# Normalised probabilities, transposed attention outputs, and high/low value products over pairs of query tiles

## The chip, the cores and the metric

One core of one Trainium2 chip runs the whole program. The metric is the device time of one execution in microseconds (us). A measurement of this kernel can tell a difference of about 0.2% from none.

## What is computed

Two blocks of two layers each work on 512 tokens with 2048 features, all in float32. The change touches the first block alone, of which each layer is (cut to what matters):

```python
def _layer(x, ...):
    h = _rms_norm(x, g_pre)
    proj = h @ w_in                      # 512 x 2048 by 2048 x 5952
    # a: 8 query heads, 2 key/value heads of 128, normed and rotated (the grouped attention)
    # b: 4 heads, keys and values from a latent of 256
    # c: 4 heads, each query sees 8 x 16 neighbours, with a bias table
    s = q @ k.T * scale
    p = softmax(s)
    o = p @ v
    o_a, o_b, o_c = (o * silu(gate) for each of the three)
    y = concat([o_a, o_b, o_c]) @ w_out  # 512 x 2048 by 2048 x 2048
    return x + _rms_norm(y, g_post)
```

The second block has another mixture (a sliding window, a spatial gate, a gated linear attention) and a modulation vector, `silu(c) @ w_mod`, which GpSimd computes while the first block runs.

## The kernel before

**The dense products.** The weights stream from HBM in panels 512 columns wide (`PW`), each as 8 pieces of two 128-row tiles (`ND`, `KC` = 16 row tiles). ScalarE rounds a piece to fp32r (`split_hi`, L1330), VectorE takes the rest (`split_lo`, L1815), and TensorE makes three matmuls per row tile and 128-token tile: high by low, high by high, low by high (`weights`, L830 to L832; L825 to L827 in the form `turned`, where the weights are the stationary side and the result comes out with features on the partitions). So a step, one row tile of a panel, is 12 matmuls of 512 columns. Panels 0 to 11 of a layer (`NIN` = 12) are `w_in`; panels 12 and on are `w_out`. Panel 2 and 3 are turned; 8 to 11 are the gates.

**The order of the work.** Each engine has its own program, written out by hand, in the same steps. `side1(l, s)` on TensorE, ScalarE and VectorE holds what is done beside the dense product at step s = 16 * panel + row tile. Tables of numbers set the steps: `UNIT_AT` (the attention units), `JOB_AT` (transposes and small products on the way to them), `SUM_AT` (sums of the modulation), `QROPE_A_AT`, `ARSQ_AT`, `ASUM_AT` (query rotation, reciprocal root and sums on VectorE). VectorE and ScalarE run the splits and the side work in one in-order stream: a piece's split, then the sides of two steps (`run`). At a gate panel's end comes `take_gate`: tanh on ScalarE, four multiplications from the banks on VectorE (`gate`, L1919), after which TensorE may use the banks again, and four of `Y` by the gate (`apply`, L1925).

**An attention unit** is one head and one tile of 128 queries; there are 64 in a layer: 16 of b, 16 of c, 32 of a. With s its step in `UNIT_AT`:

- step s: TensorE makes the scores, 128x512 (`score`, L973: three fp32r matmuls in a and c, five in b); VectorE the row maximum (`row_max`, L2109, and in a L2111); ScalarE the exponential into `probs`, with its sum in `sm` (`exp`, L1546).
- step s+2 (`UNIT_TURN`): TensorE transposes `probs` in four pieces into bank 6 (`turn`, L982), ScalarE copies it to `probsT` (`take_turn`, L1554).
- step s+4 (`UNIT_PV`): TensorE multiplies by the values into bank 7, four float32 matmuls of 128 columns with `probsT` as the stationary side (`pv`, L993), which the trace records as eight, two passes each; VectorE takes the reciprocal of the sum and multiplies 128 columns of bank 7 by it into `Y` (`finish`, L2119, L2122).

The units of a stand at steps 125 to 183, in panels 7 to 11, between the two halves' preparation: query rotation (`query_rope`, L2146 to L2152, four at steps 113 to 121, four at 133 to 146), the reciprocal root at steps 124 and 145 (`rsqrt`, L1937 to L1949, and L2264), and one transposing job per head (`job`, L953; `take_job`, L2089 and L2091).

**The output projection.** `Y` has tokens on its partitions. TensorE transposes it, 16 chunks of four 128x128 pieces (`turns_y`, L863): four chunks at step 12 of panel 11, then one in each of the first 12 steps of panel 12. ScalarE and VectorE make `act_hi` and `act_lo` of each chunk from the bank (L1493, L1978).

**GpSimd** runs the modulation (`mod_panel`: L2793 and L2800 on tiles of 512, weights by its own DMA queue) in both layers of the first block. Before panel 6 of it, it waits until the first half of the query rotation is done.

## Time and profile before

| | |
|---|---|
| median of 3 runs | 3445.77 us (3444.96 to 3445.84) |
| the profiled execution's own time | 3441.93 us |
| its span, first to last instruction | 3440.1 us |
| mean granted clock of TensorE | 0.997 of full speed |
| busy: PE, DVE, ACT, POOL | 3393.8, 1883.4, 1296.1, 1161.1 us |

PE is TensorE, DVE is VectorE, ACT is ScalarE, POOL is GpSimd. A matmul's listed length is its latency; what one costs is the distance from its start to the next one's start. In the first layer (by the starts of the first matmuls) panel 7 runs from 442.0 to 494.3 us, panel 8 to 559.7, panel 9 to 627.0, panel 10 to 688.7, panel 11 to 746.9, panel 12 to 796.0.

### The profile page before, as it was taken

How to read it: one execution, taken by the hardware profiler on the slowest of the kernel's cores; microseconds unless marked ns; L12 is line 12 of the kernel's file. 1: busy time of each engine (PE TensorE's matmuls, PEld its weight loads, DVE VectorE, ACT ScalarE, POOL GpSimd, SP SyncE). 2: the span in 40 equal slices, each digit the busy share in tenths (PEclk: the TensorE clock that was granted, in tenths of full speed). 3: DMA queues.
4: the chain of work that ended last, by engine and by line, in shares of the span. 5: the costliest groups of instructions: out<-in, count | busy, mean ns of one | idle time of the engine just before them, and what ended most of it. 6: DMA issues, size and time to landing. Idle time of an engine off the chain costs nothing.

```text
span 3440.1 us, 47703 instructions
## 1 busy us (share of the span) xinstructions
PE 3393.8 (99%) x17660; PEld 2783.0 (81%) x17660; DVE 1883.4 (55%) x3202; ACT 1296.1 (38%) x2125; POOL 1161.1 (34%) x1310
## 2 busy tenths in 40 slices
PE   8999999999999999999999999999999999999998
PEld 7778878888886788888888878877888878887887
DVE  5544577554765347665457445544547535645545
ACT  6133333333641333333347345322236435432233
POOL 0477878754007778786341000001000000001000
PEclk9999999999999999999999999999999999999999
DMA  6455544445664455444557532322446622322345
GB/s 213 147 150 163 149 150 141 145 156 187 201 217 129 141 169 158 145 146 147 167 191 221 159 62 62 101 74 74 147 155 212 186 74 62 95 68 81 123 152 185
DMA packets 225295, 490.53 MB, mean 143 GB/s; under 512 B 24254, under 2 KB 33337, under 8 KB 221224
## 3 DMA queue, kind: packets, MB, share of 16 engines
q1 hardware_dynamic: 188264, 369.13, 34.7%
q0 software_dynamic: 33632, 109.11, 10.7%
q10 hardware_dynamic: 3168, 9.24, 0.8%
q8 instruction: 141, 2.31, 0.3%
q14 instruction: 90, 0.74, 0.1%
HBM read 470.54 MB, written 20.52 MB: 143 GB/s over the span
## 4 chain that ended last, share of the span: by engine, by line
PE 94%; DVE 4%; issue 1%; ACT 1%; DMA 0%; POOL 0%; DVEq 0%; SPq 0%; ACTq 0%
PE bank L830 24%; PE bank L832 23%; PE bank L831 23%; PE bank L993 3%; PE bank L973 3%; PE bank L956 2%; PE bank L825 2%; PE bank L827 2%; PE bank L826 2%; PE bank L982 2%; PE bank L1096 1%; PE bank L1075 1%; PE bank L853 1%; PE bank L863 1%; DVE wlo L1815 1%
## 5 line engine op out<-in xcount | busy, mean ns | idle before, releaser
L830 PE MATMUL bank<-wlo,act_hi 128*128 128x512 f32 (+1 forms) x3712 | 1481.0, 399 | 7.2 <-ACT Y L1409 5.3
L832 PE MATMUL bank<-whi,act_lo 128*128 128x512 f32 (+1 forms) x3712 | 1440.1, 388 | 0.0
L831 PE MATMUL bank<-whi,act_hi 128*128 128x512 f32 (+1 forms) x3712 | 1439.0, 388 | 0.0
L1815 DVE TENSOR_TENSOR wlo<-stage,whi 128x1024 fp32r<-128x1024 f32 (+1 forms) x624 | 814.6, 1308 | 770.0 <-ACT whi L1330 757.0
L1330 ACT ACTIVATE whi<-stage 128x1024 fp32r<-128x1024 f32 (+1 forms) x624 | 649.3, 1041 | 1048.5 <-PE bank L832 899.5
L830 PEld LDWEIGHTS bank<-wlo,act_hi 128*128 128x128 f32 x3712 | 698.4, 188 | 163.6 <-issue 23.7
L832 PEld LDWEIGHTS bank<-whi,act_lo 128*128 128x128 f32 x3712 | 697.9, 188 | 148.0
L831 PEld LDWEIGHTS bank<-whi,act_hi 128*128 128x128 f32 x3712 | 699.3, 188 | 130.3
L2800 POOL TENSOR_TENSOR macc<-macc,mprod 128x512 f32<-128x512 f32 x360 | 508.8, 1413 | 68.2 <-POOL mprod L2793 68.2
L2793 POOL TENSOR_SCALAR mprod<-wmod,csil 128x512 f32<-128x512 f32 x384 | 314.6, 819 | 197.6 <-issue 77.3
L2779 POOL DMA_DIRECT2D wmod<-in_w_mod x384 | 223.2, 581 | 418.9 <-DVE zone L2152 292.3
L2875 POOL TENSOR_TENSOR zone<-zone 128x256 f32<-128x256 f32 x48 | 39.1, 815 | 376.7 <-DVE zone L2602 376.7
L2832 POOL CAST act_hi<-zone 128x256 fp32r<-128x256 f32 x64 | 32.0, 516 | 380.9 <-ACT zone L1485 380.0
L1554 ACT ACTIVATE zone<-bank 128x512 f32<-128x512 f32 x128 | 76.7, 599 | 219.2 <-PE bank L982 218.9
L2857 POOL DMA_DIRECT2D macc<-in_gla_w_gate_up x4 | 2.1, 524 | 431.3 <-DVE Y L2435 431.3
L1546 ACT ACTIVATE zone<-bank,nmx,rsq 128x512 f32<-128x512 f32 x64 | 50.0, 781 | 170.0 <-DVE nmx L2111 170.0
L825 PE MATMUL bank<-act_hi,wlo 128*128 128x512 f32 x256 | 110.0, 430 | 0.0
L2119 DVE RECIPROCAL ri<-sm 128x1 f32<-128x1 f32 x128 | 20.4, 159 | 160.2 <-PE bank L993 159.6
L993 PEld LDWEIGHTS bank<-zone 128*128 128x128 f32 x768 | 100.4, 191 | 7.5
L993 PE MATMUL bank<-zone 128*128 128x128 f32 x768 | 101.0, 274 | 0.0
L827 PE MATMUL bank<-act_lo,whi 128*128 128x512 f32 x256 | 100.1, 391 | 0.0
L826 PE MATMUL bank<-act_hi,whi 128*128 128x512 f32 x256 | 99.8, 390 | 0.0
(282 smaller groups left out, 3177.5 us busy)
## 6 DMA issues: line engine op xcount, KB each, us to landing
stage<-in_w_in SPq DMA_DIRECT2D x400, 512.0 KB, 3.7
wmod<-in_w_mod POOLq DMA_DIRECT2D x384, 256.0 KB, 3.0
stage<-in_w_out SPq DMA_DIRECT2D x192, 512.0 KB, 4.0
out<-Y SPq DMA_DIRECT2D x48, 256.0 KB, 4.7
zone<-out SPq DMA_DIRECT2D x12, 1024.0 KB, 6.6
stage<-in_w_in SPq DMA_DIRECT2D x32, 320.0 KB, 3.2
Y<-in_x SPq DMA_DIRECT2D x4, 1024.0 KB, 9.1
zone<-in_x SPq DMA_DIRECT2D x4, 1024.0 KB, 6.6
```

Of the source, the lines that this page charges most:

```text
L825: pe.matmul(out, lo_w[:, tok(t)], hi_x, start=(k == 0), stop=False)
L826: pe.matmul(out, hi_w[:, tok(t)], hi_x, start=False, stop=False)
L827: mm = pe.matmul(out, hi_w[:, tok(t)], lo_x, start=False, stop=(k == KC - 1))
L830: pe.matmul(out, hi_x, lo_w, start=(k == 0), stop=False)
L831: pe.matmul(out, hi_x, hi_w, start=False, stop=False)
L832: mm = pe.matmul(out, lo_x, hi_w, start=False, stop=(k == KC - 1))
L993: mm = pe.matmul(bank[7][:, 0:HD], probsT[:, u % 2, tok(kt)], values(br, h, kt), start=(kt == 0), stop=(kt == TT - 1))
L1330: act.activation(whi[:, c % RH, :, 0:width], stage[:, c % RS, :, 0:width], ACT.Copy)\
L1815: dve.tensor_tensor(wlo[:, c % RH, :, 0:width], stage[:, c % RS, :, 0:width], whi[:, c % RH, :, 0:width].bitcast(F32), ALU.subtract).then_ ...
L2779: pool.dma_start(wmod[:, k % 2, :], src.rearrange("o p n -> (o p) n")).then_inc(mod_landed[k % 2].sem, 16)
L2793: pool.tensor_scalar(mprod[:, :], wmod[:, k % 2, :], csil[:, k:k + 1], 0.0, ALU.mult, ALU.add)\
L2800: pool.tensor_tensor(macc[:, ring, :], macc[:, ring, :], mprod[:, :], ALU.add).then_inc(mod_added.sem, 1)
```

## The change

In the first block's two layers:

- The probabilities are divided by their sum before they are transposed: `even`, at step s+1 on VectorE, does the reciprocal and one multiplication of `probs`, 128x512, in SBUF. `turn` waits for it. `finish` is a plain copy.
- The value product is made the other way round, values stationary and `probsT` moving, so that bank 7 and then `Y` hold features on the partitions, for all three attentions.
- In a, two units (two query tiles of a head) share one product: the transposed probabilities and the values are each split in a high and a low fp32r part (`turned_low` on VectorE for each unit; `values_high`, `values_low` once in a layer), and 12 fp32r matmuls of 256 columns replace 2 times 4 in float32 (`pv_pair`). It stands one step earlier than the second unit's product did. One copy, `finish_pair`, takes both.
- The gate panels 8 to 11 run `turned`, `apply` walks `Y` in feature tiles, and `turns_y` is gone from the first block: `act_hi` and `act_lo` are made from `Y` in SBUF.
- The second reciprocal root moves from step 145 to 144, the first from 124 to 122; the last query rotation from 146 to 141; GpSimd waits before its panel 6 for the row maximum of a's first unit instead of the query rotation; the post-norm gains are loaded after piece 3 of panel 12 and after the last unit.

```diff
-AQ_AT, ASUM_AT, ARSQ_AT = (113, 131), (116, 132), (124, 145)
-QROPE_A_AT = {113: (0, 0), 115: (0, 1), 119: (0, 2), 121: (0, 3), 133: (1, 0), 136: (1, 1), 139: (1, 2), 146: (1, 3)}
+AQ_AT, ASUM_AT, ARSQ_AT = (113, 131), (116, 132), (122, 144)
+QROPE_A_AT = {113: (0, 0), 115: (0, 1), 119: (0, 2), 121: (0, 3), 133: (1, 0), 136: (1, 1), 139: (1, 2), 141: (1, 3)}
+VALUES_AT = 120, 123
+PV_AT = {}
+for s, u in UNIT_AT.items():
+    if u < U_A:
+        PV_AT[s + UNIT_PV] = (u,)
+    elif u % 2:
+        PV_AT[s + UNIT_PV - 1] = (u - 1, u)
...
+        v_hl = view(ZQ, TT, 2, A_KV * HD, of=zone_r)
+        pt_hl = view(PP + 1024, 2, SEQ, of=zone_r), view(ZT + 2560, 2, SEQ, of=zone_r)
...
             def turn(l, u):
-                pe.wait_ge(exp_done.sem, exp_done.at(0, l, u + 1))
+                pe.wait_ge(norm_done.sem, norm_done.at(0, l, u + 1))
...
-                    mm = pe.matmul(bank[7][:, 0:HD], probsT[:, u % 2, tok(kt)], values(br, h, kt),
+                    mm = pe.matmul(bank[7][:, 0:P], values(br, h, kt), probsT[:, u % 2, tok(kt)],
...
+            def pv_pair(l, u, sums):
+                _, h, _ = branch(u)
+                if u == U_A:
+                    pe.wait_ge(v_lo.sem, v_lo.at(0, l, 1))
+                pe.wait_ge(pt_done.sem, pt_done.at(0, l, u + 2))
+                pe.wait_ge(fin_done.sem, fin_done.at(0, l, u))
+                pe.wait_ge(mod_ev.sem, mod_ev.at(0, l, sums))
+                part = slice(h // 4 * HD, (h // 4 + 1) * HD)
+                for kt in range(TT):
+                    for v, p in ((1, 0), (0, 0), (0, 1)):
+                        mm = pe.matmul(bank[7][:, 0:2 * P], v_hl[:, kt, v, part], pt_hl[p][:, :, tok(kt)],
+                                       start=(kt == 0 and v == 1), stop=(kt == TT - 1 and p == 1))
+                mm.then_inc(pv_done.sem, 2)
...
-                    weights(0, l, p + 2, p, side=side1, turned=p in (2, 3), at=at)
-                weights(0, l, NIN + 2, NIN, n0=2 * KC, ahead=lambda k: turns_y(0, l, k))
+                    weights(0, l, p + 2, p, side=side1, turned=p in (2, 3) or p >= GATE0[0])
+                pe.wait_ge(fin_done.sem, fin_done.at(0, l, UNITS))
+                pe.wait_ge(mod_ev.sem, mod_ev.at(0, l, 9))
+                weights(0, l, NIN + 2, NIN, n0=2 * KC)
...
             def turned_y(blk, l):
                 def go(k):
+                    if blk == 0:
+                        act.wait_ge(gated.sem, gated.at(0, l, k + 1))
...
+                        act.activation(tiles(act_hi[:, k, :]), y_rows(k), ACT.Copy, scale=0.5).then_inc(xp_hi.sem, 1)
+                        return
...
+            def turned_low(l, u):
+                dve.wait_ge(pt_hi.sem, pt_hi.at(0, l, u - U_A + 1))
+                dve.tensor_tensor(pt_hl[1][:, u % 2, :], bank[6][:, :], pt_hl[0][:, u % 2, :].bitcast(F32), ALU.subtract)\
+                   .then_inc(pt_done.sem, 1)
+            def even(l, u):
+                dve.wait_ge(exp_done.sem, exp_done.at(0, l, u + 1))
+                dve.reciprocal(ri[:, u % 4, 0:1], sm[:, u % 4:u % 4 + 1]).then_inc(dve_link.next(), 1)
+                dve.wait_ge(dve_link.sem, dve_link.now())
+                dve.tensor_scalar(probs[:, u % 2, :], probs[:, u % 2, :], ri[:, u % 4, 0:1], None, ALU.mult)\
+                   .then_inc(norm_done.sem, 1)
...
             def side1(l, s):
+                if s in PV_AT:
+                    (finish if len(PV_AT[s]) == 1 else finish_pair)(l, PV_AT[s][0])
+                if s - 1 in UNIT_AT:
+                    even(l, UNIT_AT[s - 1])
+                if UNIT_AT.get(s - UNIT_TURN, 0) >= U_A:
+                    turned_low(l, UNIT_AT[s - UNIT_TURN])
...
-                pool.wait_ge(prep.sem, prep.at(0, l, AQ_READY + 1))
+                pool.wait_ge(max_done.sem, max_done.at(0, l, U_A + 1))
```

Where instructions stand on the engines, at three places of the first layer (the line numbers of each piece are those of its own kernel).

TensorE at step 136 (panel 8, row tile 8), the end of its dense matmuls and the side work. Before (L993 value product, L982 transposes of probabilities, L953 transposes of a query head):

```order
L831 MATMUL bank<-whi,act_hi 128x512
L832 MATMUL bank<-whi,act_lo 128x512
L993 MATMUL bank<-zone 128x128 x4
L982 MATMUL bank<-ident,zone 128x128 x4
L953 MATMUL bank<-ident,Y 128x128 x4
```

With the change (L1030 is `pv_pair`, L1004 the transposes of probabilities, L975 those of the query head):

```order
L849 MATMUL bank<-act_hi,whi 128x512
L850 MATMUL bank<-act_lo,whi 128x512
L1030 MATMUL bank<-zone_r 128x256 x12
L1004 MATMUL bank<-ident,zone 128x128 x4
L975 MATMUL bank<-ident,Y 128x128 x4
```

The product there is now that of units 36 and 37; the next step has none.

VectorE from step 133 to 134 (panel 8): the maximum of unit 37, one query rotation, a split, the side work of step 134. Before (L2119 and L2122 are `finish`):

```order
L2109 TENSOR_REDUCE nmx<-bank 128x1
L2111 TENSOR_TENSOR nmx<-nmx,rsq 128x1
L2146 TENSOR_TENSOR zone<-Y,zone 128x512
L2148 TENSOR_TENSOR zone<-Y,zone 128x8x32 x2
L2152 TENSOR_TENSOR Y<-zone 128x512
L1815 TENSOR_TENSOR wlo<-stage,whi 128x1024
L2119 RECIPROCAL ri<-sm 128x1
L2122 TENSOR_SCALAR Y<-bank,ri 128x128
L2109 TENSOR_REDUCE nmx<-bank 128x1
```

With the change (L2196 and L2198 are `even`, L2184 `turned_low`):

```order
L2161 TENSOR_REDUCE nmx<-bank 128x1
L2163 TENSOR_TENSOR nmx<-nmx,rsq 128x1
L2222 TENSOR_TENSOR zone<-Y,zone 128x512
L2224 TENSOR_TENSOR zone<-Y,zone 128x8x32 x2
L2228 TENSOR_TENSOR Y<-zone 128x512
L1864 TENSOR_TENSOR wlo<-stage,whi 128x1024
L2196 RECIPROCAL ri<-sm 128x1
L2198 TENSOR_SCALAR zone<-zone,ri 128x512
L2184 TENSOR_TENSOR zone_r<-bank,zone_r 128x512
L2161 TENSOR_REDUCE nmx<-bank 128x1
```

Between the split and the maximum stand three instructions where there were two, and two of the three are 512 wide.

VectorE before the first unit of a (steps 122 to 125). Before, two splits, the query head's job, then the reciprocal root's 12 instructions (the first is shown), and after them the first maximum:

```order
L1815 TENSOR_TENSOR wlo<-stage,whi 128x1024 x2
L2089 CAST q_hl<-bank 128x512
L2091 TENSOR_TENSOR q_hl<-bank,q_hl 128x512
L1937 TENSOR_SCALAR nv<-ss 128x16
L1939 TENSOR_SCALAR nv<-nv 128x16
```

With the change, the end of the reciprocal root (L2000, L2340), the low part of the values (L2191), a split, the job, the first maximum:

```order
L2000 SCALAR_TENSOR_TENSOR rs<-nv 128x16
L2340 TENSOR_SCALAR rsq<-rs 128x4x4
L2191 TENSOR_TENSOR zone_r<-zone,zone_r 128x4x256
L1864 TENSOR_TENSOR wlo<-stage,whi 128x1024
L2141 CAST q_hl<-bank 128x512
L2143 TENSOR_TENSOR q_hl<-bank,q_hl 128x512
L2161 TENSOR_REDUCE nmx<-bank 128x1
```

The reciprocal root no longer stands between the job and the first maximum.

## Rows read from the trace of the kernel before

**Rows 1.** The page: busy time of TensorE, and the chain that ended last

```profile
PE 3393.8 (99%) x17660; PEld 2783.0 (81%) x17660; DVE 1883.4 (55%) x3202; ACT 1296.1 (38%) x2125; POOL 1161.1 (34%) x1310
...
PE 94%; DVE 4%; issue 1%; ACT 1%; DMA 0%; POOL 0%; DVEq 0%; SPq 0%; ACTq 0%
```

**Rows 2.** Timeline of PE in panel 9: start us, us, instruction, count

```profile
560.20 0.39 PE L832 MATMUL bank<-whi,act_lo 128*128 128x512 f32 x1
...
562.24 0.39 PE L832 MATMUL bank<-whi,act_lo 128*128 128x512 f32 x1
562.47 1.05 PE L993 MATMUL bank<-zone 128*128 128x128 f32 x8
...
563.59 0.40 PE L831 MATMUL bank<-whi,act_hi 128*128 128x512 f32 x1
```

**Rows 3.** Timeline of PE: transposes of Y in panel 11, then in panel 12

```profile
736.40 0.39 PE L832 MATMUL bank<-whi,act_lo 128*128 128x512 f32 x1
736.63 1.91 PE L863 MATMUL bank<-ident,Y 128*128 128x128 f32 x16
...
738.61 0.39 PE L831 MATMUL bank<-whi,act_hi 128*128 128x512 f32 x1
...
749.56 0.39 PE L832 MATMUL bank<-whi,act_lo 128*128 128x512 f32 x1
749.79 0.60 PE L863 MATMUL bank<-ident,Y 128*128 128x128 f32 x4
...
750.46 0.39 PE L831 MATMUL bank<-whi,act_hi 128*128 128x512 f32 x1
```

**Rows 4.** Timeline of PE: fp32r matmuls of 320 columns, 13 apart

```profile
96.03 0.31 PE L830 MATMUL bank<-wlo,act_hi 128*128 128x320 f32 x1
...
97.94 0.31 PE L831 MATMUL bank<-whi,act_hi 128*128 128x320 f32 x1
```

**Rows 5.** Waits of PE: waiter <- what ended it: us in total, times, longest

```profile
PE bank L973 <- DVE q_hl L2091: 7.0, 2, 3.6
PE bank L830 <- ACT Y L1409: 5.3, 2, 3.1
```

**Rows 6.** Timeline of DVE: the first reciprocal root and the maximum behind it

```profile
480.34 0.76 DVE L1937 TENSOR_SCALAR nv<-ss 128x16 f32<-128x16 f32 x1
...
487.20 0.68 DVE L2109 TENSOR_REDUCE nmx<-bank 128x1 f32<-128x512 f32 x1
```

**Rows 7.** Timeline of DVE and of PE around step 148

```profile
575.40 0.68 DVE L2146 TENSOR_TENSOR zone<-Y,zone 128x512 f32<-128x512 f32 x1
...
579.00 0.68 DVE L2089 CAST q_hl<-bank 128x512 fp32r<-128x512 f32 x1
...
580.45 1.56 PE L973 MATMUL bank<-k_hl,q_hl 128*128 128x512 f32 x3 [3.36 <-DVE q_hl L2091]
```

**Rows 8.** Windows: us, busy of PE, PEld, DVE, ACT, POOL, granted clock, DMA

```profile
495.20:498.60 3.40, 3.40 (x10) 2.60 (x9) 0.72 (x1) 2.65 (x5) 2.29 (x3) 0.51 0.35 101
494.30:559.70 65.40, 65.36 (x344) 55.70 (x345) 42.94 (x66) 26.74 (x47) 53.77 (x60) 0.97 0.49 147
515.80:551.60 35.80, 35.80 (x193) 30.55 (x193) 29.85 (x46) 12.49 (x22) 29.80 (x32) 1.00 0.46 140
```

**Rows 9.** Forms of single lines: count, duration ns min/median/max; L1815 from two windows

```profile
L2701 DVE TENSOR_SCALAR zone<-Y,rs x2: 746/746/747, 13.1 to 13.7; 128x1024 f32<-128x1024 f32 x2
L2122 DVE TENSOR_SCALAR Y<-bank,ri x128: 349/352/354, 214.7 to 1642.7; 128x128 f32<-128x128 f32 x128
L1815 DVE TENSOR_TENSOR wlo<-stage,whi x22: 1218/1226/1227, 2700.3 to 2792.5; 128x1024 fp32r<-128x1024 f32 x22
L1815 DVE TENSOR_TENSOR wlo<-stage,whi x7: 1224/2107/2311, 505.1 to 553.6; 128x1024 fp32r<-128x1024 f32 x7
```

**Rows 10.** The page: GpSimd's dearest group

```profile
L2800 POOL TENSOR_TENSOR macc<-macc,mprod 128x512 f32<-128x512 f32 x360 | 508.8, 1413 | 68.2 <-POOL mprod L2793 68.2
```

**Rows 11.** Timeline of DVE at the end of panel 11

```profile
743.63 2.48 DVE L1978 SCALAR_TENSOR_TENSOR act_lo<-bank,act_hi 128x512 fp32r<-128x512 f32 x4
```

More of the change, by code:

```diff
@@ L466, in build, with tiles, y_rows @@
         gate_tmp1 = [view(ZT + i * PW, PW) for i in range(3)] + [view(ZV + 3 * PW, PW)]
+        def tiles(x):
+            return x.rearrange("p (t n) -> p t n", t=TT)
+        def y_rows(k):
+            r = (k + KC // 2) % KC
+            return Y[:, :, r * P:(r + 1) * P]
         def sq_a(half):
@@ L755, in _, with gains_post @@
                     in_set(0, l, p + 2, A_G0 + (p - 10) * PW)
-                out_set(0, l, NIN + 2, NIN, 0, LEAD)
-                sp.wait_ge(prep.sem, prep.at(0, l, AQ_READY + 2))
-                apart(sp)
-                spread(view(ZK, DM), io["norm_post"][bass.ds(l, 1), :], gain_in)
-                out_set(0, l, NIN + 2, NIN, LEAD)
+                def gains_post():
+                    sp.wait_ge(fin_done.sem, fin_done.at(0, l, UNITS))
+                    apart(sp)
+                    spread(view(gain_at[0], DM), io["norm_post"][bass.ds(l, 1), :], gain_in)
+                out_set(0, l, NIN + 2, NIN, between={3: gains_post})
                 layer_end(0, l)
@@ L1553, in take_turn, with values_high @@
                     act.wait_ge(pv_done.sem, pv_done.at(0, l, u - 1))
-                act.activation(probsT[:, u % 2, :], bank[6][:, :], ACT.Copy).then_inc(pt_done.sem, 1)
+                if u >= U_A:
+                    act.activation(pt_hl[0][:, u % 2, :], bank[6][:, :], ACT.Copy).then_inc(pt_hi.sem, 1)
+                else:
+                    act.activation(probsT[:, u % 2, :], bank[6][:, :], ACT.Copy).then_inc(pt_done.sem, 1)
+            def values_high(l):
+                act.wait_ge(job_done.sem, job_done.at(0, l, J_AK + A_KV))
+                act.activation(v_hl[:, :, 0, :], kv_a[:, :, A_KV * HD:2 * A_KV * HD], ACT.Copy).then_inc(v_hi.sem, 1)
             def scores_high(l, first, last):
@@ L1922, in apply @@
                     def apply(t):
-                        y = Y[:, t, col:col + PW]
+                        y, gate = Y[:, t, col:col + PW], tmp(t)
+                        if blk == 0:
+                            y, gate = Y[:, :, col + t * P:col + (t + 1) * P], tiles(gate)
                         dve.wait_ge(lin_free[t].sem, lin_free[t].at(blk, l, p + 1))
-                        dve.tensor_tensor(y, y, tmp(t), ALU.mult).then_inc(gated.sem, 1)
+                        dve.tensor_tensor(y, y, gate, ALU.mult).then_inc(gated.sem, 1)
                     for t in range(TT):
@@ L1977, in go @@
                     dve.wait_ge(xp_hi.sem, xp_hi.at(blk, l, 2 * KC + k + 1))
-                    dve.scalar_tensor_tensor(out=act_lo[:, k, :], in0=XP[k % 4][:, :], scalar=0.5,
-                                             in1=act_hi[:, k, :].bitcast(F32), op0=ALU.mult, op1=ALU.subtract)\
+                    src = y_rows(k) if blk == 0 else tiles(XP[k % 4][:, :])
+                    dve.scalar_tensor_tensor(out=tiles(act_lo[:, k, :]), in0=src, scalar=0.5,
+                                             in1=tiles(act_hi[:, k, :].bitcast(F32)), op0=ALU.mult, op1=ALU.subtract)\
                        .then_inc(xp_free.sem, 1)
```

49 lines of the change are left out of this document (28 added, 21 removed).

## The prediction

> **What bounds the kernel now.** I read the page first, then TensorE's timeline, its list of waits, and only then VectorE. The page [rows 1] shows TensorE busy for 99% of the span and holding 94% of the chain that ended last. So the sum starts from TensorE: each matmul taken off its queue is time saved, each wait added on it is time lost, and another engine counts only where TensorE waits for it. The list of waits [rows 5] shows how little is left there: two waits of panel 8's first matmul for ScalarE's copies of `Y` (5.3 us, one in each layer), and two of a score for a query head's high and low parts (7.0 us). All four lie in the stretch of the grouped attention (a). In one of them the reader sees VectorE late: the reciprocal root runs from 480.34 to 487.20 in front of the first row maximum [rows 6], and the exponential, then the copies, wait for that maximum. In the other a query rotation of 3.6 us (575.40 to 579.00) stands in front of the job whose result TensorE wants, and TensorE sits for 3.36 us [rows 7]. After three of the four waits the granted clock is at its lower level, 1.2 GHz, for 3.4 us [rows 8], as in its first window; the other two are at 580.6 and 1488.6.
>
> **Prices on TensorE.** Ten starts of 512-column matmuls lie between 560.20 and 562.24, 0.2267 us apart [rows 2]. From 562.24 to 563.59 two such distances and one value product pass: 1.35 - 0.453 = 0.90 us for a unit's product. In the same way the 16 transposes at once cost 2.21 - 0.45 = 1.76 us, and four cost 0.90 - 0.453 = 0.45 [rows 3]. Matmuls of 320 columns in fp32r are 1.91 / 13 = 0.147 us apart [rows 4].
>
> **Term 1, the transposes of Y.** In each of two layers one group of 16 and 12 groups of four go: 2 x (1.76 + 12 x 0.45) = 14.3 us. They have no cover, since TensorE does not wait there; this is worth its full price.
>
> **Term 2, value products of a.** 32 pairs replace 64 products. The trace has no fp32r matmul of 256 columns at this place. The nearest rows are 512 (0.2267) and 320 columns (0.147); the line through them gives 0.147 - 64 x 0.000415 = 0.120 us. Twelve are 1.45 us against 2 x 0.90, so a pair saves 0.35 and 32 pairs 11.2 us. The bounds are the 320-column distance (12 x 0.147 = 1.76; 1.3 us saved in all) and the transposes' distance of 0.110, the shortest here for a weight load with its matmul (1.32; 15.4 us saved). I take the line, since both its ends are of the same kind and it need go only 64 columns past one. The Trainium skill (TensorE: Matmul & The Clock Gate, Back-to-back issue gap) puts 256 columns at 262 cycles, 109 ns, by which the term would be 32 x (1.80 - 1.31) = 15.7 us; by its rule for 512 columns, 216 ns, the trace with 227 is slower, so I do not take it.
>
> **Terms at nothing.** The products of b and c swap their sides and keep eight passes of 128 columns. The gate panels run turned with the same 12 matmuls of 512. The post-norm gains now wait for the last unit (step 186), but piece 4 behind them must wait for piece 0's split at steps 14 to 15 of panel 11 anyway, and the DMA engines are busy for under half of the time [rows 8]; were that cover gone, a transfer of some us would be seen once a layer. GpSimd starts its panel 6 some 8 us later; TensorE's list of waits has no GpSimd in it, and the sum of that panel is wanted only at step 148. ScalarE (26.7 of 65.4 us in panel 8) has room for one rounding of the values.
>
> **Term 3, the old waits.** The first root now runs two steps earlier, with GpSimd quiet, so the first maximum follows its score at once: 5.3 us go. The rotation leaves the front of the job at step 148: 7.0 us go as they were, with a rest in term 4. Three stretches of 3.4 us at half clock cost 1.7 us each: 5.1. Together 17.4 us. Bounds: nothing goes, or all.
>
> Terms 1 to 3 are 42.9 us.
>
> **Term 4, new waits for VectorE.** `even` puts a 512-wide multiplication in SBUF between exponential and transposes, `turned_low` a 512-wide subtraction between the copy and the product, which has one step less. The reciprocal only moves, and the copies cost no more than the multiplications they replace. The subtraction is like act_lo's: 2.48 / 4 = 0.62 us [rows 11]. For the multiplication the nearest row is 1024 columns in 0.746 us [rows 9], while GpSimd was idle: 0.37 at best. What contention adds is the question. Rows 9 show it on L1815, which reads two SBUF tiles: 1.22 us with GpSimd idle, 2.11 in the median beside it; L2122, which reads a bank, never leaves 0.35. So the lower bound is 0.37, the upper 0.37 + 1.41, a whole GpSimd addition [rows 10]. I take 0.8: half of L1815's 0.88 on top. The Trainium skill (SBUF, Who interferes with whom) says that a VectorE operation in a two-port mode and one of GpSimd lock each other out for their whole length; the two L1815 rows agree that the wait is there. By it each `even` could cost 1.8 us; that is the third rival.
>
> Where does it hurt? In panel 8, from 515.8 to 551.6 (the maxima of units 36 to 42), VectorE is busy for 29.85 of 35.8 us [rows 8]. Seven multiplications (5.6) and seven subtractions (4.3) come in, the three pair copies save 0.6: 9.3 us for 5.95 us of idle time, of which TensorE's own gain takes 1.0. So VectorE falls some 4.4 us behind, the rotation moved to step 141 takes the idle time after it, and I put 5 us of TensorE's waiting on panel 8, per layer (bounds 0, if its lag of a step absorbs it, and 10). At step 148 the job, without the rotation but with `even` in front, ends about 1.5 us after TensorE wants it. At the edge of panel 12 four low parts stand before the gate that frees the banks [rows 11]; they now read two SBUF tiles, and the transposes that gave TensorE 0.45 us of other work are gone: 0.8 us (bounds 0.1 and 3.6). Elsewhere 0.7. That is 8.0 us a layer, 16 in all.
>
> **Sum.** 42.9 - 16 = 26.9 us less, against the profiled execution's 3441.9: 3415.0. The median of the runs shown lies 3.8 above that execution, so the forecast is **3419 us**.
>
> **Rivals.** *All covered*: VectorE is idle for a third of panel 8, and its order may put the new work where it waits anyway; ScalarE's copy at least is made at once after most turns. Then 3441.9 - 42.9 + 3.8 = 3403. Against it speaks the packed stretch above. Chance 0.20.
>
> *Waits only change places*: what the moves free, `even` and `turned_low` fill, and the four old waits with their slow clock stay beside the new ones: 14.3 + 11.2 - 16 = 9.5 us less, 3436. For it speaks that the same engine serves both. Chance 0.13.
>
> *VectorE bounds the grouped attention* (slower): its place is the pair `even`, `turned_low` in panels 8 to 11. If each multiplication waits for GpSimd's addition, a unit brings 1.8 + 0.6 us to VectorE; nine units make panel 8 some 42.9 + 22 + 3.6 = 68 us for VectorE against TensorE's 62. The lag then outlives the one step between `even` and the transposes, and every unit pays. At 0.75 us for each of 64 units 48 us come on top of the forecast: 3467. It decides once a unit's loss passes 0.42 us. Against it: panels 9 to 11 have more room, and GpSimd is not at work all the time. Chance 0.06.
>
> *The wide products are no cheaper*: 256 columns cost as 320, so term 2 is 1.3 us: 3429. Chance 0.08.
>
> **How the numbers follow.** The forecast has 0.53. A measurement of this kernel tells 0.2% (6.9 us) from no change, so faster means under 3438.9. The forecast, all covered and the wide products lie there (0.81), and most of the places rival; with tails of the forecast beyond it I say 0.86 faster, 0.08 same, 0.06 slower. The range 3402 to 3438 reaches to the covered and the places rival; outside it are half of the former, the slower case, and a little more.
>
> **What the new profile would show.** L863's successor with 128 instead of 256 transposes. Twelve matmuls of 256 columns start 1.45 us before the next work. Panel 12 shorter by 5.4 us and panel 11 by 1.8 and more. In the list of waits of TensorE, waits for VectorE's normalised `probs` or low parts of some 10 us, mostly in panel 8, and less than 4 us for the query head. The multiplication in `even` at 0.4 to 1.8 us, median about 0.8. I am wrong if panels 8 to 11 do not get shorter, if the 256-column distance is 0.147 or more, or if TensorE's waits in the first block pass 30 us.

## The result, and the profile after

| | before | after |
|---|---|---|
| median of 20 runs each | 3445.84 us (3441.01 to 3450.49) | 3452.51 us (3442.80 to 3460.49) |
| ratio, 95% interval | 1 | 1.0019 [1.0012, 1.0026] |
| profiled execution: own time, span | 3441.93, 3440.1 us | 3448.19, 3446.4 us |
| mean granted clock | 0.997 | 0.995 |

The change makes the kernel 0.19% slower; the interval lies clear of 1, but the difference is no larger than what such a measurement can tell at all. The prediction was 3419 us, with 0.86 on faster. A trace shows one execution, and that of the changed kernel was 4.3 us below its median. The page of after stands against [rows 1] as follows.

```profile
PE 3379.5 (98%) x17404; PEld 2762.4 (80%) x17404; DVE 1997.2 (58%) x3364; ACT 1295.7 (38%) x2127; POOL 1160.3 (34%) x1310
...
PE 88%; DVE 7%; issue 3%; ACT 1%; DMA 0%; POOL 0%; DVEq 0%; another core or an unknown queue 0%; ACTq 0%; SPq 0%; POOLq 0%
```

TensorE has 256 fewer instructions and 14 us less busy time, and yet the span is 6 us longer: the chain has lost 6 points of TensorE and won 3 of VectorE and 2 of issue. VectorE has 114 us more. So the work was saved, and more than the saving was lost in waits. The list of waits says where:

```profile
PE bank L1004 <- DVE zone_r L2184: 9.1, 9, 2.5
...
PE bank L853 <- DVE zone L1968: 5.6, 2, 2.8
...
PE bank L1030 <- issue: 4.5, 2, 2.3
PE bank L848 <- DVE zone L1968: 4.3, 2, 2.7
PE bank L995 <- DVE q_hl L2143: 3.6, 6, 0.7
PE bank L1004 <- DVE zone L2198: 3.3, 4, 1.4
PE bank L1030 <- DVE zone_r L2184: 2.9, 2, 1.8
```

Of the two old pairs of waits [rows 5] one is gone (the copies of `Y`) and one is halved (3.6 us for the query head in place of 7.0). In their place the transposes (L1004) wait for a low part: 9.1 us in nine times. They cannot start before `turned_low` (L2184) of the unit before has read bank 6, since that signal, `pt_done`, now comes from VectorE and no longer from ScalarE's copy. The pair product (L1030) waits for the same signal, and the first dense matmul after a gate panel (L848, L853) for the gate (L1968). By the starts of the first matmuls the panels last, in us:

| panel | 7 | 8 | 9 | 10 | 11 | 12 |
|---|---|---|---|---|---|---|
| before, layer 0 | 52.3 | 65.4 | 67.3 | 61.7 | 58.2 | 49.1 |
| after, layer 0 | 48.4 | 77.9 | 63.1 | 61.2 | 60.0 | 45.2 |
| before, layer 1 | 50.8 | 63.8 | 66.9 | 61.8 | 58.2 | 49.1 |
| after, layer 1 | 48.5 | 74.4 | 65.0 | 61.3 | 60.0 | 44.9 |

Panel 8 alone loses 12.5 and 10.6 us, and it should have become shorter. One wait in its first steps, in the timeline of PE and then of DVE:

```profile
496.68 0.39 PE L850 MATMUL bank<-act_lo,whi 128*128 128x512 f32 x1
499.35 1.50 PE L1030 MATMUL bank<-zone_r 128*128 128x256 f32 x9 [2.28 <-issue]
```

```profile
495.54 2.27 DVE L1864 TENSOR_TENSOR wlo<-stage,whi 128x1024 fp32r<-128x1024 f32 x1 [1.89 <-ACT whi L1361]
497.74 0.15 DVE L2196 RECIPROCAL ri<-sm 128x1 f32<-128x1 f32 x1
497.92 0.73 DVE L2198 TENSOR_SCALAR zone<-zone,ri 128x512 f32<-128x512 f32 x1
498.57 0.67 DVE L2184 TENSOR_TENSOR zone_r<-bank,zone_r 128x512 fp32r<-128x512 f32 x1
```

The wait that the trace calls "issue" is one for VectorE: the pair product starts at 499.35, 0.1 us after the low part ends, and that stood behind a split of 2.27 us (the split before it took 1.23) and `even`. The split had itself waited 1.89 us for ScalarE's rounding, which stood behind an exponential that had waited 1.82 us for VectorE's row maximum: with three engines in order, a delay of VectorE comes back to it. The gate panel's end shows the other kind. Before, four low parts of the activations (`act_lo`) from a bank took 2.48 us there [rows 11]; now

```profile
747.20 5.18 DVE L2030 SCALAR_TENSOR_TENSOR act_lo<-Y,act_hi 128x512 fp32r<-128x512 f32 x4
752.30 1.87 DVE L1968 SCALAR_TENSOR_TENSOR zone<-zone,bank 128x512 f32<-128x512 f32 x3
```

and TensorE's first matmul of panel 12 waits for 2.82 us. Behind such waits the granted clock falls to its lower level, 1.2 GHz (windows: us, busy of PE, PEld, DVE, ACT, POOL, clock, DMA):

```profile
500.30:503.70 3.40, 3.40 (x14) 3.11 (x14) 1.12 (x2) 1.33 (x2) 2.87 (x4) 0.50 0.48 160
...
752.90:756.30 3.40, 3.18 (x8) 2.53 (x9) 3.40 (x7) 0.02 (x1) 2.87 (x4) 0.50 0.26 82
```

Seven such stretches stand in the first block of after (from 500.3, 527.6, 558.3, 752.9, 1439.0, 1479.9 and 1664.2) where before has three. TensorE had waited 1.84 to 2.82 us shortly before each; behind a wait of 2.27 us at 1410.3 none came. The price of the pair product, on the other hand, is as forecast:

```profile
516.11 1.60 PE L1030 MATMUL bank<-zone_r 128*128 128x256 f32 x12
517.54 0.86 PE L995 MATMUL bank<-k_hl,q_hl 128*128 128x512 f32 x3
```

1.43 us from its start to the next work, against the 1.45 of term 2.

### The profile page after: what moved, and what is told of

It is laid out like the page before. It is cut to its first block, busy times and chain, and to the rows that moved or that the text cites. A ratio compares the mean times of both kernels' runs of the same rounds, so it can differ in the third digit from the quotient of the medians.

```text
span 3446.4 us, 47369 instructions
## 1 busy us (share of the span) xinstructions
PE 3379.5 (98%) x17404; PEld 2762.4 (80%) x17404; DVE 1997.2 (58%) x3364; ACT 1295.7 (38%) x2127; POOL 1160.3 (34%) x1310
## 4 chain that ended last, share of the span: by engine, by line
PE 88%; DVE 7%; issue 3%; ACT 1%; DMA 0%; POOL 0%; DVEq 0%; another core or an unknown queue 0%; ACTq 0%; SPq 0%; POOLq 0%
PE bank L853 21%; PE bank L855 20%; PE bank L854 20%; PE bank L848 4%; PE bank L850 4%; PE bank L849 4%; PE bank L995 3%; PE bank L978 2%; PE bank L1015 2%; DVE wlo L1864 2%; PE bank L1004 1%; PE bank L1127 1%; PE bank L1030 1%; PE bank L1106 1%; PE bank L876 1%
## 5 line engine op out<-in xcount | busy, mean ns | idle before, releaser
L853 PE MATMUL bank<-wlo,act_hi 128*128 128x512 f32 (+1 forms) x3200 | 1273.9, 398 | 7.5 <-DVE zone L1968 5.6
L855 PE MATMUL bank<-whi,act_lo 128*128 128x512 f32 (+1 forms) x3200 | 1239.7, 387 | 0.0
L854 PE MATMUL bank<-whi,act_hi 128*128 128x512 f32 (+1 forms) x3200 | 1239.3, 387 | 0.0
L853 PEld LDWEIGHTS bank<-wlo,act_hi 128*128 128x128 f32 x3200 | 602.2, 188 | 145.8 <-issue 24.0
L2882 POOL TENSOR_TENSOR macc<-macc,mprod 128x512 f32<-128x512 f32 x360 | 510.7, 1419 | 68.2 <-POOL mprod L2875 68.2
L848 PE MATMUL bank<-act_hi,wlo 128*128 128x512 f32 x768 | 315.5, 411 | 4.3 <-DVE zone L1968 4.3
L850 PE MATMUL bank<-act_lo,whi 128*128 128x512 f32 x768 | 301.4, 392 | 0.0
L849 PE MATMUL bank<-act_hi,whi 128*128 128x512 f32 x768 | 301.1, 392 | 0.0
L848 PEld LDWEIGHTS bank<-act_hi,wlo 128*128 128x128 f32 x768 | 145.8, 190 | 41.2 <-issue 13.3
L850 PEld LDWEIGHTS bank<-act_lo,whi 128*128 128x128 f32 x768 | 145.1, 189 | 32.3
L849 PEld LDWEIGHTS bank<-act_hi,whi 128*128 128x128 f32 x768 | 145.7, 190 | 31.2 <-issue 3.3
L1585 ACT ACTIVATE zone<-bank,nmx 128x512 f32<-128x512 f32 x64 | 44.1, 688 | 136.6 <-DVE nmx L2165 70.9
```

The costliest lines, as they stand in the source:

```text
L848: pe.matmul(out, lo_w[:, tok(t)], hi_x, start=(k == 0), stop=False)
L849: pe.matmul(out, hi_w[:, tok(t)], hi_x, start=False, stop=False)
L850: mm = pe.matmul(out, hi_w[:, tok(t)], lo_x, start=False, stop=(k == KC - 1))
L853: pe.matmul(out, hi_x, lo_w, start=(k == 0), stop=False)
L854: pe.matmul(out, hi_x, hi_w, start=False, stop=False)
L855: mm = pe.matmul(out, lo_x, hi_w, start=False, stop=(k == KC - 1))
```

## The experiments

The theory was, to begin with: VectorE's new work, `turned_low` above all since bank 6 hangs on it, holds TensorE in panel 8. Its rivals: `even` does it; the moved steps do it; GpSimd's work beside VectorE does it. Each run was timed against the kernel before; the changed kernel stands at 1.0019.

**Steps alone.** The kernel before with nothing but the moved steps: both roots, the last rotation and GpSimd's wait.

```diff
-AQ_AT, ASUM_AT, ARSQ_AT = (113, 131), (116, 132), (124, 145)
+AQ_AT, ASUM_AT, ARSQ_AT = (113, 131), (116, 132), (122, 144)
... (QROPE_A_AT: the last rotation, (1, 3), from step 146 to 141)
-                pool.wait_ge(prep.sem, prep.at(0, l, AQ_READY + 1))
+                pool.wait_ge(max_done.sem, max_done.at(0, l, U_A + 1))
```

> The kernel before with nothing but the moved steps: reciprocal roots at 122 and 144, the last query rotation at 141, GpSimd's panel 6 after the first row maximum. Term 3 of the prediction says that the two old pairs of waits (12.3 us) and three stretches at half clock (5.1 us) go: 3446 - 17.4 = about 3428 us. The rival (the waits only change places: the rotation put at step 141 stands in front of other work of VectorE) says within 5 us of 3446 us, with panel 8 longer than 65.4 us and panel 9 shorter than 67.3.

Measured: 3428.42 us, ratio 0.9953 [0.9940, 0.9965]. 17.0 us less than the runs of before beside it (3445.46), by the forecast 17.4. Panel 7 lasts 48.4 us in both layers, panel 9 61.9 and 61.8. Panel 8, which now holds all four rotations, lasts 66.4 and 64.4 where it had 65.4 and 63.8: the rival's mark shows, but for 1.5 us against 10 won in panel 9. The moves are a full gain by themselves; the rest of the change therefore costs 3452.5 - 3428.4 = 24 us. They have a price on VectorE all the same. Its busy time in panel 8 (the third of the row) is 47.92 us here and was 42.94 [rows 8]:

```profile
489.90:556.30 66.40, 64.42 (x346) 54.24 (x344) 47.92 (x72) 27.40 (x47) 53.95 (x60) 1.00 0.45 134
```

**Without high and low value products.**

```diff
-    if u < U_A:
-        PV_AT[s + UNIT_PV] = (u,)
-    elif u % 2:
-        PV_AT[s + UNIT_PV - 1] = (u - 1, u)
+    PV_AT[s + UNIT_PV] = (u,)
...
+                act.activation(probsT[:, u % 2, :], bank[6][:, :], ACT.Copy).then_inc(pt_done.sem, 1)
...
-                if UNIT_AT.get(s - UNIT_TURN, 0) >= U_A:
-                    turned_low(l, UNIT_AT[s - UNIT_TURN])
```

> The change without its high and low value products: in the grouped attention each unit has again its own product of four float32 matmuls (0.90 us on TensorE), at step s+4, and turned_low, values_high and values_low are gone; even, the turned gate panels and the moved steps stay. TensorE gets 11.2 us of work back (32 pairs x 0.35). If turned_low is what holds TensorE (64 x 0.68 us on VectorE and bank 6 kept until it is done), panel 8 of the first layer falls from 77.9 to about 68 us, most of the 49 us of new waits go (25 to 30 of them) and the time is 3452.5 + 11 - 28 = about 3435 us. If it is even that holds TensorE, the waits stay, panel 8 stays above 75 us and the time is about 3463 us.

Measured: 3429.61 us, ratio 0.9950 [0.9937, 0.9962]. Although TensorE has 11 us more to do, the kernel is 23 us faster than the change, so the low parts and the pair product cost 34 us of waiting (slow clock included). Panel 8 lasts 68.2 and 68.4 us. Waits for `even` (L2191 in this kernel) and the gate (L1961) are left:

```profile
PE bank L851 <- DVE zone L1961: 6.0, 2, 3.2
PE bank L1002 <- DVE zone L2191: 4.9, 4, 1.7
...
PE bank L846 <- DVE zone L1961: 2.9, 2, 1.6
```

**Chunks of the output projection earlier.** The first four of `act_hi` and `act_lo` go out of panel 11's end into the side work of step 188.

```diff
+                def with_chunks(l, s):
+                    side1(l, s)
+                    if s == 188:
+                        four(turned, 0)
                 for p in range(8, NIN):
-                    panel(0, l, p, take_gate(0), side=side1, ahead=(lambda: four(turned, 0)) if p == NIN - 1 else None)
+                    panel(0, l, p, take_gate(0), side=with_chunks)
... (the same on ScalarE)
```

> The change with the first four chunks of act_hi and act_lo made in the side work of step 188 (panel 11, row tile 12) instead of behind panel 11's last split. If act_lo in front of the gate is what makes TensorE wait at panel 12 (2.8 us and 1.7 us of half clock a layer), the time falls by 9 us to about 3443 us, and the wait of TensorE for the gate at panel 12 is gone. The rival: the 5.2 us of act_lo stand in front of a split of panel 11 instead, and TensorE waits there: within 3 us of 3452 us, panel 11 longer by what panel 12 gains.

Measured: 3444.64 us, ratio 1.0000 [0.9991, 1.0008]; 7.9 us less than the change. Panels 11 and 12 last 57.0 and 43.6 us in place of 60.0 and 45.2, in both layers, 9.0 us together. The wait did not move into panel 11: in the timeline of DVE the four fit in idle time, before a split that had to wait for ScalarE anyway. But in this trace panels 9 and 10 are longer than in the changed kernel's, by 1.3 to 2.3 us each, though the edit touches nothing there; no run says why.

```profile
744.03 2.49 DVE L2034 SCALAR_TENSOR_TENSOR act_lo<-Y,act_hi 128x512 fp32r<-128x512 f32 x4
747.55 1.23 DVE L1868 TENSOR_TENSOR wlo<-stage,whi 128x1024 fp32r<-128x1024 f32 x1 [1.04 <-ACT whi L1361]
```

They also took 2.49 us here, not 5.18, on the same two SBUF tiles: by the windows (columns as above, here first after, from 747.2 us, then this kernel) GpSimd was busy for 4.38 of 5.20 us there, and is quiet here, as it waits for a load.

```profile
747.20:752.40 5.20, 3.10 (x14) 2.25 (x12) 5.20 (x6) 4.76 (x9) 4.38 (x5) 1.00 0.46 151
```

```profile
744.00:746.50 2.50, 2.50 (x13) 2.07 (x12) 2.50 (x5) 0.21 (x2) 0.00 (x0) 1.00 0.91 346
```

Part of the gain may be luck: which engine is quiet at 744 us was not planned.

**The multiplication on ScalarE.**

```diff
-                dve.tensor_scalar(probs[:, u % 2, :], probs[:, u % 2, :], ri[:, u % 4, 0:1], None, ALU.mult)
+                act.activation(probs[:, u % 2, :], probs[:, u % 2, :], ACT.Copy, scale=ri[:, u % 4, 0:1])
```

> The change with the multiplication of the probabilities by the reciprocal made by ScalarE (Copy with a scale) at the same step; VectorE keeps the reciprocal alone, so it loses 128 multiplications, some 30 to 40 us each layer. If the amount of VectorE's work is the cause of the new waits, panels 8 and 9 of the first layer (141 us together) fall by 10 us or more and the time to about 3430 us. If the cause is the longer chain between exponential and transposes, or turned_low behind rotations and splits, this engine change gives nothing: within 5 us of 3452 us, with waits for ScalarE or for turned_low in their place.

Measured: 3484.70 us, ratio 1.0116 [1.0100, 1.0131]. Both times missed, the 3430 and the 3452; it is 32 us slower than the change. Only the second's waits for `turned_low` did come. VectorE has 84 us less to do (1912.9), and TensorE waits more, even in the profiled execution, the fastest of the four (3470.78 us):

```profile
PE bank L1005 <- DVE zone_r L2192: 24.7, 18, 3.1
...
PE bank L1031 <- issue: 6.4, 2, 3.3
```

In this kernel ScalarE, in order, stands still until VectorE has the reciprocal (196.9 us in 119 waits), and what is queued behind it, the copy of the transposes among it, comes late: VectorE's idle time in front of `turned_low` grows from 22.1 us to 62.2. Panel 8 of the first layer is as long as in the changed kernel, with 6.4 us less work on VectorE (53.78 for 60.16):

```profile
491.70:569.20 77.50, 65.31 (x326) 53.37 (x324) 53.78 (x77) 34.29 (x57) 63.49 (x72) 0.98 0.43 129
```

The load of VectorE is thus not the whole cause; the chain VectorE to ScalarE to TensorE to ScalarE to VectorE within two steps counts as well.

**Without the multiplication of `even`.**

```diff
-                dve.tensor_scalar(probs[:, u % 2, :], probs[:, u % 2, :], ri[:, u % 4, 0:1], None, ALU.mult)\
-                   .then_inc(norm_done.sem, 1)
```

> The change without the multiplication in even (the reciprocal stays, the probabilities of the first block are left without their division). The run with single products has put some 34 us on the low parts (3452 to 3430 with 11 us more on TensorE); if the rest of the waits is even's, panel 8 still falls from 77.9 to 70 us or less here, because the multiplication stands in front of each low part, and the time to about 3430 us. If even lies in idle time of VectorE, nothing moves: 3448 to 3452 us.

Measured: 3430.70 us, ratio 0.9956 [0.9943, 0.9968]. Panel 8 lasts 69.3 and 73.0 us, so the 70 came true in the first layer alone. Taking away the multiplication of `even` gives 22 us, taking away the low parts 34 (with the dearer products counted). The two overlap: together they would be more than the 49 us lost in new waits, so it is no single one of them. The first form of the theory, that `turned_low` does it, falls; what counts is the queue of both.

**Without GpSimd's arithmetic**, in the changed kernel and in the one before.

```diff
-                    pool.tensor_scalar(mprod[:, :], wmod[:, k % 2, :], csil[:, k:k + 1], 0.0, ALU.mult, ALU.add)\
-                        .then_inc(mod_used.sem, 1)
+                    pool.sem_inc(mod_used.sem, 1)
-                        pool.tensor_tensor(macc[:, ring, :], macc[:, ring, :], mprod[:, :], ALU.add).then_inc(mod_added.sem, 1)
+                    pool.sem_inc(mod_added.sem, 1)
```

> The change with GpSimd's arithmetic for the modulation left out (the multiplications and additions of the weights; its loads, signals and TensorE's sums stay, so the modulation vector is missing from the result). If VectorE is late because GpSimd's work lengthens its splits and multiplications, the waits of panels 8 to 11 (49 us) nearly go: panel 8 of the first layer falls from 77.9 to 64 us or less, and the time is about 3452 - 40 = 3412 us. If VectorE is late by the amount and order of its own work, panel 8 stays above 72 us and the time above 3435 us.

> The kernel before with the same arithmetic of GpSimd left out. Its two waits for ScalarE's copies (5.3 us) and part of the two for the query head go, with their half clock: 3445 - 10 = about 3435 us. If GpSimd is the cause of the change's new waits, the changed kernel without it is 20 us or more below this one (terms 1 and 2 alone are 25.5 us); if it is not, the two stay within 10 us of each other.

Measured: the changed kernel 3396.87 us, ratio 0.9857 [0.9842, 0.9872]; the kernel before 3420.90 us, 0.9928 [0.9915, 0.9940]. Without GpSimd's arithmetic the change is worth 24.0 us, and of the waits for `even`, the low parts and the gate TensorE's list keeps 1.0 us, two of the "issue" at the pair product. The difference lies panel by panel where terms 1 and 2 put it: 0.8, 1.4, 1.4, 2.9 and 5.5 us for panels 8 to 12 of the first layer, 12.0 together. I expected 10 us for the kernel before and it was 24.8: the 17 of the moves (panels 7 and 9), and in the two layers together 2.9 us in panel 2 and 1.7 in panel 8, which I had not seen as GpSimd's.

The windows of panel 8 of the first layer show what GpSimd does to VectorE (columns as above): first after, then the kernel before and the changed one, both without the arithmetic.

```profile
490.90:568.80 77.90, 68.03 (x326) 55.99 (x324) 60.16 (x86) 27.43 (x48) 64.43 (x72) 0.93 0.43 129
```

```profile
488.50:552.20 63.70, 63.70 (x345) 54.52 (x344) 34.02 (x68) 25.79 (x45) 12.34 (x23) 1.00 0.54 167
```

```profile
489.30:552.20 62.90, 62.39 (x326) 52.51 (x325) 44.54 (x86) 25.81 (x45) 15.84 (x29) 1.00 0.59 182
```

Without GpSimd's arithmetic the change adds 44.54 - 34.02 = 10.5 us to VectorE in panel 8, the moved rotation (2.1 us) among it; my 9.3 was for seven units in 35.8 us of the panel, with contention. Beside GpSimd the panel's work is 42.94 us before [rows 8] and 60.16 after: GpSimd added 8.9 us before, and adds 15.6 after. With the steps alone it adds 47.92 - 34.02 - 2.1 = 11.8, so 2.9 of the 6.7 us more come with the fourth rotation. The list by form, 490 to 700 us, after and then after without the arithmetic (busy us, mean ns), shows which instructions bear it:

```profile
L1864 DVE TENSOR_TENSOR wlo<-stage,whi 128x1024 fp32r<-128x1024 f32 x26 | 43.3, 1667 | 18.0 <-ACT whi L1361 17.9
L2184 DVE TENSOR_TENSOR zone_r<-bank,zone_r 128x512 fp32r<-128x512 f32 x27 | 18.4, 682 | 9.1 <-ACT zone_r L1594 9.1
...
L2198 DVE TENSOR_SCALAR zone<-zone,ri 128x512 f32<-128x512 f32 x26 | 16.7, 642 | 0.9
...
L2163 DVE TENSOR_TENSOR nmx<-nmx,rsq 128x1 f32<-128x1 f32 x25 | 8.9, 355 | 0.9
...
L2228 DVE TENSOR_TENSOR Y<-zone 128x512 f32<-128x512 f32 x4 | 5.6, 1408 | 0.1
```

```profile
L1865 DVE TENSOR_TENSOR wlo<-stage,whi 128x1024 fp32r<-128x1024 f32 x28 | 34.2, 1222 | 23.4 <-ACT whi L1362 23.4
L2185 DVE TENSOR_TENSOR zone_r<-bank,zone_r 128x512 fp32r<-128x512 f32 x29 | 19.9, 687 | 19.5 <-ACT zone_r L1595 19.5
...
L2199 DVE TENSOR_SCALAR zone<-zone,ri 128x512 f32<-128x512 f32 x28 | 13.7, 489 | 1.0
...
L2164 DVE TENSOR_TENSOR nmx<-nmx,rsq 128x1 f32<-128x1 f32 x28 | 4.5, 160 | 1.0
...
L2229 DVE TENSOR_TENSOR Y<-zone 128x512 f32<-128x512 f32 x4 | 2.8, 692 | 0.1
```

`turned_low`, which reads a bank, is the same beside GpSimd and without. Without GpSimd's arithmetic the multiplication of `even` is 0.15 us shorter. The old instructions with two SBUF tiles gain most: the split 0.45, the rotation's last addition 0.72, and even a product of two columns 0.20.

**The two-column product in another form.**

```diff
-                    dve.tensor_tensor(nm, m, rsq[:, t, h:h + 1], ALU.mult).then_inc(max_done.sem, 1)
+                    dve.tensor_scalar(nm, m, rsq[:, t, h:h + 1], None, ALU.mult).then_inc(max_done.sem, 1)
```

> The change with one instruction of the row maximum written otherwise: the product of two columns (128x1) of the grouped attention is a tensor_scalar with the second column as its scalar, no longer a tensor_tensor of two SBUF tiles. The tensor_tensor took 0.16 us without GpSimd's arithmetic and 0.36 us in the mean beside it, up to 0.84. If operations with two SBUF tiles wait for GpSimd and those with one do not, it takes 0.16 us always, VectorE wins 5 us a layer, and with it TensorE about as much: 3452 - 8 = 3444 us. If what waits is any operation of VectorE, its mean stays at 0.36 us and the time at 3452 us.

Measured: 3446.76 us, ratio 0.9997 [0.9988, 1.0005], 0.22% or some 7.6 us under the change. The line's forms, of after and of this kernel (duration ns min/median/max):

```profile
L2163 DVE TENSOR_TENSOR nmx<-nmx,rsq x64: 158/178/842, 483.6 to 1637.8; 128x1 f32<-128x1 f32 x64
```

```profile
L2163 DVE TENSOR_SCALAR nmx<-nmx,rsq x64: 212/214/217, 483.9 to 1635.7; 128x1 f32<-128x1 f32 x64
```

The form itself is dearer than I thought (0.214 against 0.16 us), but beside the same GpSimd it never waits. The Trainium skill (SBUF, Who interferes with whom) says just this: an operation of VectorE with at most one SBUF input, outside the two-port modes, does not contend with GpSimd, one with two contends with GpSimd's reads. The rows of both forms, and those of `turned_low`, agree. The form alone does not free an instruction: the multiplication of `even`, with one tile and a column too, takes 485 to 1402 ns beside GpSimd (median 594) and 485 to 670 without (487), and one of the root's `tensor_scalar`, 16 columns wide, took 1261 ns for 169. Whether these are two-port modes no run here tells.

**A pause of GpSimd.**

```diff
+                    if (p, k) == (6, 8):
+                        pool.wait_ge(max_done.sem, max_done.at(0, l, 41))
```

> The change with GpSimd stopped in the middle of its panel 6 (after half of its row tiles) until the row maximum of unit 40, which is some 25 us of quiet in the stretch of panel 8 where the query rotations stand; all its work is still done. If GpSimd's work beside VectorE is what makes VectorE late there, panel 8 of the first layer falls from 77.9 to about 70 us, and the time to 3452 - 14 = about 3438 us. If GpSimd only has to be somewhere and every place costs the same, or if TensorE then waits for the sum at step 148: within 4 us of 3452 us.

Measured: 3437.56 us, ratio 0.9972 [0.9962, 0.9983], some 16 us under the change, all of GpSimd's work being done. Panel 8 lasts 70.9 and 69.2 us (77.9 and 74.4). Panel 9 of the first layer gets longer, 67.1 us for 63.1, so a part came back there. By the panels of both layers, 12.1 us are won in panel 8 and 6.3 lost in panels 9 and 10: the same additions of GpSimd cost less there than among the rotations. Another 7.6 us are won in panels 11 and 12, which were not forecast; the four low parts at the edge take 4.03 us in place of 5.18.

**Both versions with the three edits** (chunks earlier, the two-column product, the pause).

> The change with three edits: the first four chunks of act_hi and act_lo at step 188, the one-column product as a tensor_scalar, and GpSimd's pause. By the sum of the three, 8 + 8 + 14 us: 3422 us, if they add. If the low parts behind rotations and splits hold TensorE all the same: 3435 us or more.

> The same three edits on the kernel with float32 products unit by unit. Without low parts there is less left to win: panel 8 is at 67.9 and 65.2 us against 63.7 without GpSimd, panel 9 at 65.7 and 62.6 against 61.8. 3422.8 - 6 = about 3417 us. If the pair product is worth its 11.2 us once VectorE has room, this one is not below the pair version with the same edits.

Measured: with pair products 3423.08 us, ratio 0.9931 [0.9918, 0.9945], the sum as forecast, though not piece by piece: the pause had won 7.6 us in panels 11 and 12 and the chunks 9.0, and together they win 12.6 there. With float32 products unit by unit **3410.20 us, 0.9890 [0.9877, 0.9904]**. The latter beats the kernel before by 1.1%, and is 1.3% under the changed one by the ratios. In its panel 8 TensorE does not wait at all:

```profile
490.10:553.90 63.80, 63.80 (x346) 54.47 (x345) 44.41 (x80) 26.20 (x46) 34.22 (x39) 1.00 0.38 112
```

The pair version has 68.7 us there, and in both layers together 5.4 us of waits for the gate of panel 8 and 9 us for low parts. So the pair product, 11 us cheaper on TensorE, still makes this kernel 13 us slower.

**Float32 products with the chunks earlier.**

> The two edits that gained, together: float32 products unit by unit at step s+4, and the first four chunks of act_hi and act_lo at step 188. The gains come at different places, so they should add: 3429.6 - 8 = about 3421 us, with no wait for the gate at panel 12. If the four chunks only move the wait into panel 11, as half of it did in the changed kernel, 3426 us.

Measured: 3422.78 us, ratio 0.9931 [0.9919, 0.9944]; the gains add, less 1 to 2 us.

**The order of the low part and `even`**, in the change and in the pair version with the three edits.

```diff
-                if s - 1 in UNIT_AT:
-                    even(l, UNIT_AT[s - 1])
                 if UNIT_AT.get(s - UNIT_TURN, 0) >= U_A:
                     turned_low(l, UNIT_AT[s - UNIT_TURN])
+                if s - 1 in UNIT_AT:
+                    even(l, UNIT_AT[s - 1])
```

> The change with turned_low ahead of even in VectorE's side work of a step; nothing else. If the place in VectorE's queue decides, a low part comes 0.65 us earlier, TensorE's waits for it (12.0 us in the list) and the issue at the pair product shrink, and the time falls to about 3446 us. If the amount decides, the normalised probabilities come later by the low part and the wait for ScalarE's copy in front of it, and the time stays within 4 us of 3452 us or rises.

> The same swap in the pair version with the three edits (3423 us). There VectorE has more room, so that the low parts wait for ScalarE's copy rather than for VectorE. By the place: about 3418 us. By the amount: 3421 to 3427 us. If even now waits behind a low part that waits for a copy, waits of TensorE for even appear and it is slower, 3430 us or more.

Measured: 3476.30 us, ratio 1.0079 [1.0065, 1.0093], and 3433.14 us, 0.9957 [0.9944, 0.9969]: by the ratios 21 us slower in the one, 9 in the other. The first outcome had been left open ("or rises"), the second is the third case named. The waits for the low part turn into waits for `even`, and become more. In the change with the swap:

```profile
PE bank L1004 <- DVE zone L2198: 26.6, 18, 3.6
...
PE bank L1030 <- DVE zone_r L2184: 3.2, 3, 1.2
```

A low part in front waits for ScalarE's copy of the same step (49.6 us of VectorE's idle time in place of 22.1), and `even`, which could have been done meanwhile, waits with it. The order in the change is the better one.

## Why the prediction was wrong, point by point

- **Term 1** (transposes, 14.3 us) holds. Without GpSimd's arithmetic panel 12 falls from 49.1 to 43.6 us, 5.5 for the 5.4 forecast.
- **Term 2** (pairs, 11.2 us) holds: 1.43 us where I had 1.45, and the line between 320 and 512 columns was the right choice of the three. Terms 1 and 2 together were 25.5 us, measured 24.0 without GpSimd's arithmetic. The rival of the wide products is out.
- **Term 3** (old waits, 17.4 us) holds: 17.0 by itself.
- **Term 4** (new waits, 16 us) is the step that failed. 3445.8 - 42.9 is 3403, and the result is 3452.5: 49 us lost in waits and their slow clock. The list of waits has 33.3 us of it, the slow stretches 11.9. By panels, against the changed kernel without GpSimd's arithmetic: panel 8 is 15.0 and 11.6 us longer in the two layers (I had 5, at most 10), panels 11 and 12 together 6.2 and 5.9 (I had 0.8 for their edge, at most 3.6), panel 9 2.6 and 4.6, panel 10 0.8 and 0.9.
- Within it, **"what contention adds is the question"** was asked of `even` alone. The size taken for it was not too low: its median is 0.594 us, below my 0.8, and its longest 1.40, below the bound of 1.78; only the lower bound was wrong, since half the columns did not take half of 0.746 us: the shortest took 0.485. The rows of L1815 were also the wrong ones for it, as that instruction reads two SBUF tiles and `even` one. What I left out is what GpSimd does to the old instructions: its share of VectorE's busy time in panel 8 went from 8.9 to 15.6 us. By the rows of that panel 3.7 of the 6.7 us stand in the rotations, of which the moved step brings a fourth into it, 1.7 in `even` and some 0.6 in the two-column products. My account, 9.3 us of work for 5.95 us of idle time, had of all this only the share of `even`.
- **"VectorE falls some 4.4 us behind, and I put 5 us on panel 8"** took the lag as paid once. It is paid at each point where TensorE, in order, needs one result: bank 6 after each low part, the pair product, the gate. I had seen that the product has one step less, but not that `turn` of the next unit waits for `turned_low` of this one, because `pt_done` changed its engine. The run without low parts takes this tie and the low parts' own time away together, for 34 us; what each is worth by itself no run shows.
- **The edge of panel 12** was at 0.8 us; it is a wait of 2.8 us with a slow clock behind it, twice, and the kernel with the chunks moved is 7.9 us faster. Its upper bound had the right mechanism, four low parts from two SBUF tiles, and I chose the low end.
- **The slow clock** was counted for the waits that go (5.1 us) and not for those that come. Seven stretches came where three went: at 1.7 us each, 11.9 us for which term 4 has no line.
- **The rivals.** *VectorE bounds the grouped attention*, at 0.06 and 3467 us, is the nearest: its place was right, its price of 1.8 us for each `even` was not (0.594 in the median), since the queue and not a single wait does it. *All covered* is refuted with GpSimd at work, and its number, 3403, is near what the change gives without it (3396.87), where some 7 us of the kernel's other losses are gone as well. *Waits only change places* is refuted by the list of waits, in which 3.6 of the 12.3 us of old waits are left, and by the run of the steps alone.
- The marks named at the end did show it: panels 8 to 11 got longer (262.2 us for 252.6 in the first layer), and TensorE's waits in the first block passed 30 us (33.3 in the list).

How the 49 us split between low parts, `even` and GpSimd has no single answer, as each of the three, taken away, gives 20 us or more, and they sum to more than the whole. How a pair product would do with a second bank for the transposes, and how the change would do with its last rotation left at step 146, were not tried.

## What to carry to other kernels

Before work is put on a helping engine, add up that engine's busy time in the stretch with its contention, not per new instruction: in panel 8, VectorE busy for 43 to 45 us went with a loss of at most 1.7 us, 48 with 2.6, 51 with 4.5, 59 and 60 with 12 and 15. The chain counts beside the amount: with the multiplication on ScalarE 54 us went with 15 as well. Look at which engine gives the signal that frees a shared bank; moving it from one engine to another puts the bank behind all that stands in that engine's queue. And when two changes come together, time the cheap one alone: here a few moved steps were 17 us of gain, hidden under 24 us of loss.

## What the hardware showed that was not expected

- A product of two columns, one element on each partition, takes 0.159 us without GpSimd's arithmetic and up to 0.842 us beside it, 0.355 in the mean in panels 8 to 10. The wait is thus not in proportion to the instruction's own length. With one column as the scalar operand it took 0.212 to 0.217 us in all 64.
- GpSimd's arithmetic in the first block costs the kernel before 24.8 us and the changed one 55.6 us (3452.5 - 3396.9), though GpSimd is never in TensorE's list of waits.
- Four low parts from two SBUF tiles took 5.18 us beside GpSimd and 2.49 us while it waited for a load, so one place in a program can have either price.
- Taking 84 us of work from VectorE and giving it to ScalarE made the kernel 32 us slower.
- Executions lie far apart where TensorE waits much, and close where it does not: 17.7 us over 20 of the changed kernel, 1.1 us over four of it without GpSimd's arithmetic, 2.2 us over four of the float32 version with the three edits.
